# Cross-attention products of weights and values as three fp32r passes instead of one fp32 product

## The reference, cut to what matters

```python
def cross_attn(h, memn, w_q, w_k, w_v, w_o):
    B, T, _ = h.shape
    q = (h @ w_q).reshape(B, T, CROSS_HEADS, CROSS_DH)
    k = (memn @ w_k).reshape(B, MEM_LEN, CROSS_HEADS, CROSS_DH)
    v = (memn @ w_v).reshape(B, MEM_LEN, CROSS_HEADS, CROSS_DH)
    s = jnp.einsum('bqhd,bkhd->bhqk', q, k).astype(jnp.float32) * (CROSS_DH ** -0.5)
    p = jax.nn.softmax(s, axis=-1).astype(v.dtype)
    o = jnp.einsum('bhqk,bkhd->bqhd', p, v).reshape(B, T, D_MODEL)
    return o @ w_o
```

## Time and profile before

| what | value |
|---|---|
| median of three runs | 1619.91 us |
| the profiled execution, own time | 1619.36 us |
| its span (first to last instruction) | 1617.3 us |
| PE busy in the span | 1593.6 us (99%) |
| DVE busy | 721.0 us (45%) |
| ACT busy | 670.3 us (41%) |
| POOL busy | 794.6 us (49%) |
| mean granted clock of TensorE, of full speed | 0.997 |

### The profile page before, as it was taken

How to read it: one execution, slowest core, us unless ns; L and a number is a source line. 1 busy time by engine, 2 the same in 40 slices (tenths; PEclk the granted TensorE clock), 3 DMA queues, 4 the chain that set the end, 5 groups by cost and what they waited for, 6 DMA issues and landing times. The chain is left out here.

```text
span 1617.3 us, 22551 instructions
## 1 busy us (share of the span) xinstructions
PE 1593.6 (99%) x7646; PEld 1292.0 (80%) x7646; DVE 721.0 (45%) x1370; ACT 670.3 (41%) x1079; POOL 794.6 (49%) x1060
## 2 busy tenths in 40 slices
PE   7999999999999999999999999999999999999997
PEld 6787777777888888888888878778978888888886
DVE  5497996664233212121132444653223651452354
ACT  5424685554334323232233434643543442333332
POOL 5244573333555455545554542256635465565553
PEclk9999999999999999999999999999999999999998
DMA  5222222113332232323233321133323223223231
GB/s 182 92 79 78 79 91 79 53 57 103 102 101 95 91 104 91 104 91 104 91 101 103 108 77 53 53 104 113 122 70 100 91 91 104 91 94 106 86 104 65
DMA packets 45077, 149.78 MB, mean 93 GB/s; under 512 B 4616, under 2 KB 7824, under 8 KB 45008
## 3 DMA queue, kind: packets, MB, share of 16 engines
q1 hardware_dynamic: 38592, 139.48, 26.7%
q10 hardware_dynamic: 6416, 9.36, 1.7%
HBM read 146.58 MB, written 2.11 MB: 92 GB/s over the span
## 5 line engine op out<-in xcount | busy, mean ns | idle before, releaser
L300 POOL TENSOR_TENSOR w_lo<-w_raw,w_hi 128x256 fp32r<-128x256 f32 x1056 | 794.4, 784 | 798.5 <-ACT w_hi L915 797.8
L329 PE MATMUL job<-a_hi,w_hi 128*128 128x512 f32 (+1 forms) x1056 | 406.5, 385 | 10.1 <-POOL w_lo L300 10.1
L331 PE MATMUL job<-a_hi,w_lo 128*128 128x512 f32 (+1 forms) x1056 | 398.4, 377 | 0.0
L330 PE MATMUL job<-a_lo,w_hi 128*128 128x512 f32 (+1 forms) x1056 | 398.2, 377 | 0.0
L915 ACT ACTIVATE w_hi<-w_raw 128x1024 fp32r<-128x1024 f32 x264 | 274.9, 1050 | 276.6 <-PE job L331 269.3
L329 PE MATMUL job<-b_hi,w_hi 128*128 128x512 f32 x952 | 375.4, 394 | 0.4 <-DVE b_lo L1439 0.4
L331 PE MATMUL job<-b_hi,w_lo 128*128 128x512 f32 x952 | 370.9, 390 | 0.0
L330 PE MATMUL job<-b_lo,w_hi 128*128 128x512 f32 x952 | 370.5, 389 | 0.0
L329 PEld LDWEIGHTS job<-a_hi,w_hi 128*128 128x128 f32 x1056 | 199.2, 189 | 52.5 <-DVE a_lo L1439 10.8
L330 PEld LDWEIGHTS job<-a_lo,w_hi 128*128 128x128 f32 x1056 | 199.4, 189 | 37.2 <-issue 1.9
L331 PEld LDWEIGHTS job<-a_hi,w_lo 128*128 128x128 f32 x1056 | 199.1, 189 | 37.1
(11 more groups left out here) (271 smaller groups left out, 1359.8 us busy)
## 6 DMA issues: line engine op xcount, KB each, us to landing
w_raw<-w_all SPq DMA_DIRECT2D x264, 512.0 KB, 3.5
arena<-x_t ACTq DMA_DIRECT2D x8, 512.0 KB, 5.9
arena<-rg_w ACTq DMA_DIRECT2D x1, 1024.0 KB, 6.5
arena<-row_table ACTq DMA_DIRECT2D x2, 512.0 KB, 4.3
arena<-mem_t ACTq DMA_DIRECT2D x1, 1024.0 KB, 6.5
out_t<-arena SPq DMA_DIRECT2D x4, 256.0 KB, 2.4
out_t<-arena ACTq DMA_DIRECT2D x4, 256.0 KB, 2.5
arena<-consts ACTq DMA_DIRECT2D x1, 384.0 KB, 4.0
```

The lines of the kernel that those rows point to most:

```text
L300: nc.gpsimd.tensor_tensor(w_lo[:, sl, c], raw[:, sl, c], w_hi[:, sl, c].bitcast(F32), ALU.subtract).then_inc(s("lo_ready"), 1)
L329: mm(ps[:, 0:n], w_hi[:, sl, c], hi[:, kt, 0:n], start=kt == 0, stop=False)
L330: mm(ps[:, 0:n], w_hi[:, sl, c], lo[:, kt, 0:n], start=False, stop=False)
L331: ins = mm(ps[:, 0:n], w_lo[:, sl, c], hi[:, kt, 0:n], start=False, stop=kt == last)
```

## The change

The product of weights and values is no longer made by fp32 matmuls but, like the jobs, by three fp32r passes over high parts and rests. For this

- ACT's copies out of `t_ps` now write high parts: the weights into `b_hi` (which the jobs J_QC have left free), the values into columns 256 to 511 of `a_hi`. The arena tiles `c_v` and `c_pt` are gone;
- DVE makes the rests from the same PSUM banks: `probabilities_low` (two subtractions of 128x512 for each head) into `b_lo`, `cv_low` (one for each head) into columns 256 to 511 of `a_lo`. That is 12 new instructions, and PE waits for them where it waited for ACT's copies (`cr_pt_lo` for `cr_pt`, and `cv_ready` is now raised by DVE);
- the values of head c lie in the tiles of `a_hi` and `a_lo` into which the high parts and rests of the head's product go, so `high_values(c)` waits for both halves of the product (`cr_pv` at 2c + 2) before it writes the first.

```diff
-        c_v = flat(tiles(12, 4)).rearrange("p (e c) -> p e c", c=D)
+        cv_hi, cv_lo = a_hi[:, :, MEM:T], a_lo[:, :, MEM:T]
...
             def turn_values(c):
                 pe.wait_ge(s("job_taken"), J_MEM + 8 + 2 * c + 2)
-                pe.wait_ge(s("cr_pt"), 2 * min(c + 2, 4))
+                pe.wait_ge(s("cr_pt_lo"), 2 * min(c + 2, 4))
...
                 if c >= 1:
-                    pe.wait_ge(s("cr_pt"), 2 * c)
+                    pe.wait_ge(s("cr_pt_lo"), 2 * c)
...
                     for e in range(2):
-                        ins = mm(job_ps[k][:], c_v[:, e, (2 * c + k) * P:(2 * c + k + 1) * P], c_pt[c][e],
-                                 start=e == 0, stop=e == 1)
+                        n, r = 2 * c + e, slice(k * P, k * P + P)
+                        mm(job_ps[k][:], cv_hi[:, n, r], b_hi[:, n, :], start=e == 0, stop=False)
+                        mm(job_ps[k][:], cv_hi[:, n, r], b_lo[:, n, :], start=False, stop=False)
+                        ins = mm(job_ps[k][:], cv_lo[:, n, r], b_hi[:, n, :], start=False, stop=e == 1)
                     ins.then_inc(s("cr_pv"), 1)
...
             def high_values(c):
+                act.wait_ge(s("cr_pv"), 2 * c + 2)
                 for k in range(2):
-                    act.wait_ge(s("cr_pv"), 2 * c + k + 1)
                     fn(a_hi[:, 2 * c + k, :], job_ps[k][:], ACT.Copy).then_inc(s("chi_ready"), 1)
...
+            def probabilities_low(c):
+                for e in range(2):
+                    dve.wait_ge(s("cr_pt"), 2 * c + e + 1)
+                    tt(b_lo[:, 2 * c + e, :], t_ps[e][:], b_hi[:, 2 * c + e, :].bitcast(F32), ALU.subtract).then_inc(
+                        s("cr_pt_lo"), 1)
+
+            def cv_low(c):
+                dve.wait_ge(s("cv_high"), c + 1)
+                tt(cv_lo[:, 2 * c:2 * c + 2, :], t_ps[0][:].rearrange("p (e c) -> p e c", c=2 * P),
+                   cv_hi[:, 2 * c:2 * c + 2, :].bitcast(F32), ALU.subtract).then_inc(s("cv_ready"), 1)
...
             take_keys(7, 1)
-            take_values(0, 2)
+            take_values(0, 1)
             cross_inverse(1)
+            probabilities_low(0)
+            take_values(1, 1)
             cross_max(2)
-            take_values(2, 2)
+            take_values(2, 1)
+            probabilities_low(1)
+            take_values(3, 1)
             cross_inverse(2)
+            cv_low(0)
             cross_max(3)
-            take_values(4, 2)
+            take_values(4, 1)
+            probabilities_low(2)
+            take_values(5, 1)
             cross_inverse(3)
-            take_values(6, 2)
-            for c in range(4):
+            cv_low(1)
+            take_values(6, 1)
+            probabilities_low(3)
+            take_values(7, 1)
+            cv_low(2)
+            low_values(0)
+            cv_low(3)
+            for c in range(1, 4):
                 low_values(c)
```

More of the change, by code:

```diff
@@ L215, in build @@
         c_k = flat(tiles(8, 4)).rearrange("p (k c) -> p k c", c=MEM)
-        c_v = flat(tiles(12, 4)).rearrange("p (e c) -> p e c", c=D)
+        cv_hi, cv_lo = a_hi[:, :, MEM:T], a_lo[:, :, MEM:T]
         c_p = [flat(tiles(i, 2)).rearrange("p (n c) -> p n c", c=MEM) for i in (22, 24)]
-        c_pt = [[arena[:, i, :] for i in pair] for pair in ((20, 21), (26, 27), (0, 1), (2, 3))]
         c_vt = flat(tiles(16, 4)).rearrange("p (k c) -> p k c", c=MEM)
@@ L1335, in take_turned @@
                     act.wait_ge(s("cr_turn"), 2 * c + e + 1)
-                    fn(c_pt[c][e], t_ps[e][:], ACT.Copy).then_inc(s("cr_pt"), 1)
+                    fn(b_hi[:, 2 * c + e, :], t_ps[e][:], ACT.Copy).then_inc(s("cr_pt"), 1)
             def take_values(c):
                 act.wait_ge(s("cv_turned"), c + 1)
-                fn(c_v[:, :, 2 * c * P:(2 * c + 2) * P], t_ps[0][:].rearrange("p (e c) -> p e c", c=2 * P),
-                   ACT.Copy).then_inc(s("cv_ready"), 1)
+                fn(cv_hi[:, 2 * c:2 * c + 2, :], t_ps[0][:].rearrange("p (e c) -> p e c", c=2 * P),
+                   ACT.Copy).then_inc(s("cv_high"), 1)
             def high_values(c):
+                act.wait_ge(s("cr_pv"), 2 * c + 2)
                 for k in range(2):
-                    act.wait_ge(s("cr_pv"), 2 * c + k + 1)
                     fn(a_hi[:, 2 * c + k, :], job_ps[k][:], ACT.Copy).then_inc(s("chi_ready"), 1)
```

## The result

The changed kernel takes 1624.52 us (median of 9 runs, 1624.01 to 1624.91), the kernel before, measured beside it, 1619.96 us (9 runs, 1619.58 to 1620.35). The ratio is 1.0027, 95% interval 1.0019 to 1.0036: slower by 4.6 us. The forecast was 1624.6. The profiled execution took 1624.28 us itself. A second profiled execution of the same kernel is 0.18 us behind there.

What follows compares the result with a forecast made beforehand. PE, busy 99% of the span, was taken as the bound. Passes -2.88, the pair's wait +6.45 and turns +1.12 gave +4.69 us on the profiled 1619.36, 1624.05; with the median 0.55 above, 1624.6 us, range 1622.2 to 1626.8.

Steps and rivals of the forecast that it cites:

- What bounds the kernel: Whole kernel: PE, busy 99% of the span, so its gains and losses count in full and nothing later gives any back.
- The pair's wait, 6.45 us: Between heads' products: ACT copies only after both halves, so PE waits 1.29 + 3 x 1.72 = 6.45 us.
- The four places: PE was to wait ahead of heads 1, 2 and 3 and ahead of J_OC.
- the discount for `turn_values(3)`: Ahead of head 1, its 0.43 us lies in the wait and was paid before, so 1.29 us are lost, not 1.72.
- The passes, -2.88 us: Products of weights and values: 48 fp32r passes at 0.227 us replace 32 at 0.430, saving PE 2.88 us.
- the bound (2.72): Lower bound for the passes' saving, 2.72 us, from 0.23 us a pass in J_OC's own first passes.
- The turns, 1.12 us: Turning of weights and values: PE waits for DVE's new subtractions, 1.12 us late in all, bounds 0 and 1.7.
- the three places named: PE was to wait for DVE at `turn_values(0)`, `turn_values(1)` and `turn_probabilities(3)`, late by 0.43, 0.91 and 1.12 us.
- The sum, +4.69: At J_OC's start: -2.88 + 6.45 + 1.12 = +4.69 us, moving it from 1199.4 to 1204.1.
- The rival of the clock: Loop over heads: pauses lower PE's clock, 1627.3 us if for one head, 1635 for all four; chance 6%.
- The rival of cheap turns and restarts: Turns cost 0 and each restart 0.15 us less as PE loads ahead: +2.97, 1622.9 us; chance 12%.
- The rival of winning passes: Products: the 2.88 us saving outweighs everything, the pair's wait being mostly covered; 1618.2 us without waits; chance 3%.

Runs made afterwards that it cites:

- the wait alone: Kernel before, fp32 products kept, only ACT's copies of a head's halves made to wait for both halves: 1626.67 us, ratio 1.0040.
- its removal: Changed kernel with the products of heads 1 and 3 in two other PSUM banks: 1617.89 us, ratio 0.9987.
- The two kernels with four banks: Changed kernel with heads 1 and 3 in two other PSUM banks, 1617.89 us; the same plus values turned in score banks, 1615.83 us.
- the earlier reciprocal: Changed kernel with DVE's inverses of heads 2 and 3 ahead of the rests of the head before: 1623.39 us, run again 1623.06 us.
- The values apart: Changed kernel with the values turned into score banks instead of the bank the weights use too: 1622.56 us, ratio 1.0018.
- the old products with both bank edits: Kernel before, fp32 products, with heads 1 and 3 in two other banks and values turned in score banks: 1618.97 us, ratio 0.9997.

## Why the prediction was right

By its own steps:

- *What bounds the kernel*: right. PE's loss went into the time in full, and nothing behind gave any back.
- *The pair's wait, 6.45 us*: right in size (6.46 by the wait alone, 6.45 by its removal) and in cause. Its composition was measured too: 0.19 to ACT's start, 0.63, 0.69, and 0.23 until PE streams. The four places and the discount for `turn_values(3)` came as forecast.
- *The passes, -2.88 us*: right in kind, a little too large. The piece grew by 3.75, so with 6.46 of waits the passes brought 2.71. The forecast took 0.227 us, which is the distance in a long run of passes (after, two takes of J_OC are again 5.44 us apart); these come in groups of 12 and are 0.230 apart. 48 x 0.003 is 0.14 of the missing 0.17. The nearer row was J_OC's own first passes, named as the bound (2.72) and not taken.
- *The turns, 1.12 us*: the term that was mis-sized. They cost 0.84. The waits are at the three places named, but `turn_values(0)` loads 0.13 late where 0.43 was forecast, and the other two carry this 0.3 on (0.56 for 0.91, 0.83 for 1.12). The step that failed is "ACT's two copies run 1164.78 to 1165.87", taken as before, and with it "DVE subtracts the first at 1165.41". In the changed kernel the copies start at 1164.93, which is 0.36 us earlier when the 0.51 are taken off. The prediction went by where the new subtractions stand and passed over an old instruction that moves: `cross_inverse(1)` now stands ahead of the taking of the second values. DVE's reciprocal of head 1 starts at 1153.68 instead of 1156.90, relative 3.73 earlier; ACT's next split follows (1157.14 instead of 1158.72), and POOL's subtractions behind it. With POOL's work at another place a tiny DVE instruction ahead of ACT's copies became shorter (the last section says how far this is shown).
- *The sum, +4.69*: measured +4.59 and +4.56 at J_OC in two executions. The errors of the two terms, +0.17 and -0.28, partly cancel.
- *The rival of the clock*: refuted here. The granted clock is 1.00 in the stretch with four pauses of up to 1.7 us, and from 1184 to 1210 in both traces of the changed kernel and in the seven of the experiments that were taken at full clock. The clock falls at the end only, as before. The Trainium skill, "TensorE: Matmul & The Clock Gate", "A second HAM failure mode: psum-queue depth-cycling", describes a swing of the clock from such short idles; no trace here shows it at these pauses.
- *The rival of cheap turns and restarts*: its turns were half met (0.84 of 1.12), its restarts not at all: PE does not load weights ahead of the wait (the load at 1195.41 follows the rest written at 1195.29), and a restart took 0.23 where 0.20 was worked out.
- *The rival of winning passes*: with the waits taken away it is what happens. The two kernels with four banks are faster than before. It failed here for the reason given: nothing covers 1.3 us of copies once both halves must be finished.

Of the experiments' expectations one failed in size and in part in its reason, that of the earlier reciprocal. The values apart gained 0.5 us more than expected by the median and 0.2 by the trace (1.62 for 1.4).

## What to carry to other kernels

Price a wait by what covered it before: the same ACT and DVE work cost nothing beside four passes, 1.7 us a time without them, and nothing again once PE had two more banks. When a cheaper form of the work needs its inputs for longer, as here where the result overwrites the values, look for the buffer that must be free next, and rotate it, before counting the saving. To size such a pause, add the legs of the chain from rows (end of PE to ACT, ACT to DVE, the subtraction, the restart), and take the distance of passes from a short group and not from a long run. List the old instructions whose place changes as well as the new ones: one reciprocal that moved up shifted the work of ACT and POOL, and the wait of PE changed with it.

## What the runs showed of the hardware

**A tiny DVE instruction gets long beside POOL.** DVE's TENSOR_SCALAR on 128x4 numbers, SBUF to SBUF, which ends the maxima of a head, takes 0.17 us in some places and up to 0.70 in others. It is on the path: the exponentials wait for it. DVE and POOL in order of time, in the kernel before:

```profile
1156.90 0.17 DVE L1970 RECIPROCAL small<-small 128x4 f32<-128x4 f32 x1
1161.34 0.65 DVE L1446 TENSOR_SCALAR small<-small 128x4 f32<-128x4 f32 x1
1171.84 0.69 DVE L1446 TENSOR_SCALAR small<-small 128x4 f32<-128x4 f32 x1
```

```profile
1150.34 8.44 POOL L300 TENSOR_TENSOR w_lo<-w_raw,w_hi 128x256 fp32r<-128x256 f32 x12 [4.30 <-ACT w_hi L915]
1159.84 2.83 POOL L300 TENSOR_TENSOR w_lo<-w_raw,w_hi 128x256 fp32r<-128x256 f32 x4 [1.05 <-ACT w_hi L915]
1170.38 2.83 POOL L300 TENSOR_TENSOR w_lo<-w_raw,w_hi 128x256 fp32r<-128x256 f32 x4 [2.59 <-ACT w_hi L915]
```

POOL's subtractions of 128x256 follow one another about 0.70 us apart. The third of the group from 1159.84 ends at 1161.96, DVE's instruction at 1161.99; the third of the group from 1170.38 ends at 1172.51, DVE's at 1172.53. In the changed kernel the reciprocal stands earlier, POOL's group runs on without a gap and ends at 1162.10, and DVE's instruction is short:

```profile
1153.68 0.17 DVE L1971 RECIPROCAL small<-small 128x4 f32<-128x4 f32 x1
1161.86 0.27 DVE L1447 TENSOR_SCALAR small<-small 128x4 f32<-128x4 f32 x1
```

```profile
1150.86 11.24 POOL L299 TENSOR_TENSOR w_lo<-w_raw,w_hi 128x256 fp32r<-128x256 f32 x16 [4.29 <-ACT w_hi L916]
```

And in the kernel with the reciprocals of heads 2 and 3 earlier POOL is idle when the second one comes, and it takes 0.17:

```profile
1172.04 0.17 DVE L1447 TENSOR_SCALAR small<-small 128x4 f32<-128x4 f32 x1
```

```profile
1168.88 2.79 POOL L299 TENSOR_TENSOR w_lo<-w_raw,w_hi 128x256 fp32r<-128x256 f32 x4 [1.34 <-ACT w_hi L916]
```

This fits both sizes that were off: 0.38 us less at the first (0.65 to 0.27) beside the 0.36 by which ACT's copies came earlier, and 0.44 less at the second (0.61 in the changed kernel to 0.17) beside the 0.41 of idle time that vanished. It holds beyond these traces. The instruction occurs 40 times in the ten traces taken at full clock. In 29 of them a POOL instruction is under way when it starts, and it ends 0.02 to 0.03 us after that one; in the 11 others it takes 0.17. The first of the two takes 0.65 to 0.66 us in the three kernels with the reciprocal of head 1 at its old place, and 0.21 to 0.28 in the seven traces with it at its new one (the three are also those with the old products). Not every tiny instruction is held up: the RECIPROCAL at 1156.90, on numbers of the same size, takes its 0.17 us beside a busy POOL, and in all 38 such places of these traces 0.17 to 0.18. That the earlier reciprocals take away the second wait is shown, since nothing else was changed in that kernel; the way through POOL is read from the traces, and no kernel moved POOL's work alone. The Trainium skill, "SBUF — State Buffer", "Terms", states that DVE and GpSimd arbitrate for a shared pair of ports, which one of them holds for a whole instruction while the other blocks. The traces agree with that for the TENSOR_SCALAR, in where it ends, and show nothing of it for the RECIPROCAL.

**The first passes of a row** of fp32r passes of 128x512 are 0.224 to 0.236 us apart from the second on, 0.229 to 0.231 in the mean of a head's twelve, and later in a long row 0.227. It is not the pause that does it: head 0 of the changed kernel follows a turn without a pause (0.229), and in the old products with both bank edits J_OC follows fp32 products without a wait, with eight distances of 0.231 in the mean from 1199.00 to 1200.85. Why was not tried.
